# Adding three weight sums by transfers, scaling a token tile by itself, and reordering work at the output projection

## What is computed

```
h    = rms_norm(x, g_pre)                        # 512 x 2048
proj = h @ w_in                                  # 512 x 7174
out_a = moba_attention(qa, ka, va, rel_bias)     # 6 heads of 128, causal, relative bias
out_b = forgetting_attention(qb, kb, vb, log_f)  # 6 heads, bias from cumulated log forget gates
km, vm = split(rms_norm(mem, g_mem) @ w_mem_kv)  # 256 memory tokens
out_m = memory_attention(qm, km, vm)             # 4 heads
y = concat(out_a * silu(ga), out_b * silu(gb), out_m * silu(gm))
o = y @ w_out                                    # 512 x 2048 times 2048 x 2048
return x + rms_norm(o, g_post)
```

## Time and profile before

| | |
|---|---|
| median of three runs | 887.97 us |
| profiled execution | 889.66 us |
| its span on the core | 887.9 us |
| PE busy | 865.6 us, 97% |
| DVE busy | 727.2 us, 82% |
| ACT busy | 536.8 us, 60% |
| POOL busy | 75.9 us, 9% |
| mean granted clock of PE | 0.994 |

### The profile page before, as it was taken

One profiled execution on the slowest core, in us unless ns is written; L12 is line 12 of the kernel. 1 busy time (PEld: TensorE's weight loads), 2 busy tenths in 40 slices (PEclk: granted clock), 3 DMA queues, 4 the chain that ended last, 5 costly groups with the idle time before them and its releaser, 6 DMA issues.

```text
span 887.9 us, 13757 instructions
## 1 busy us (share of the span) xinstructions
PE 865.6 (97%) x5181; PEld 766.0 (86%) x5181; DVE 727.2 (82%) x1025; ACT 536.8 (60%) x918; POOL 75.9 (9%) x84
## 2 busy tenths in 40 slices
PE   9998999999999999999999999999999989999995
PEld 6997999988888888888888888888888878778884
DVE  5799789988888888888888888888888886975558
ACT  6795556565656565656565656565656575654452
POOL 0000310000000000000030303030301000000000
PEclk9999999999999999999999999999999999999999
DMA  9980586567668577657677768577644597466845
GB/s 289 303 200 23 165 181 165 148 172 159 160 171 196 137 178 176 161 163 177 153 183 170 165 171 185 144 185 170 161 121 107 172 366 259 146 214 208 289 190 189
DMA packets 179143, 161.37 MB, mean 182 GB/s; under 512 B 7353, under 2 KB 144217, under 8 KB 177670
## 3 DMA queue, kind: packets, MB, share of 16 engines
q1 hardware_dynamic: 170166, 142.66, 52.6%
q0 software_dynamic: 8704, 16.78, 13.7%
q10 hardware_dynamic: 208, 1.07, 0.4%
HBM read 152.33 MB, written 43.28 MB: 220 GB/s over the span
## 4 chain that ended last, share of the span: by engine, by line
PE 78%; DVE 12%; ACT 6%; issue 4%; DVEq 0%; POOL 0%; ACTq 0%; POOLq 0%
PE d_ps L709 19%; PE d_ps L714 10%; PE e_ps L709 10%; PE e_ps L714 5%; PE c_ps L709 5%; PE pt_ps L819 3%; DVE ring L1482 3%; PE d_ps L658 3%; PE c_ps L714 2%; PE d_ps L659 2%; PE d_ps L660 2%; ACT ring L1032 2%; PE score_ps L659 2%; PE score_ps L658 2%; PE score_ps L660 2%
## 5 line engine op out<-in xcount | busy, mean ns | idle before, releaser
L1482 DVE TENSOR_TENSOR ring<-raw,ring 128x1024 fp32r<-128x1024 f32 x134 | 164.5, 1230 | 48.6 <-ACT ring L1032 48.5
L1482 DVE TENSOR_TENSOR ring<-sums,ring 128x1024 fp32r<-128x1024 f32 x112 | 137.5, 1227 | 51.2 <-ACT ring L1032 51.1
L1032 ACT ACTIVATE ring<-raw 128x1024 fp32r<-128x1024 f32 x134 | 140.7, 1055 | 41.5 <-PE d_ps L660 15.4
L709 PE MATMUL d_ps<-late,ring 128*128 128x512 f32 x576 | 145.1, 394 | 0.0
L1032 ACT ACTIVATE ring<-sums 128x1024 fp32r<-128x1024 f32 x112 | 118.1, 1054 | 16.3 <-DVE sums L1509 13.1
L709 PEld LDWEIGHTS d_ps<-late,ring 128*128 128x128 f32 x576 | 103.4, 189 | 18.5
L714 PEld LDWEIGHTS d_ps<-late,ring 128*128 128x128 f32 x576 | 78.6, 190 | 5.7
L714 PE MATMUL d_ps<-late,ring 128*128 128x256 f32 x576 | 80.2, 282 | 0.0
L1509 DVE TENSOR_TENSOR sums<-raw 128x1024 f32<-128x1024 f32 x56 | 68.7, 1227 | 0.1
L1509 DVE TENSOR_TENSOR sums<-sums,raw 128x1024 f32<-128x1024 f32 x56 | 68.5, 1223 | 0.0
L2057 POOL DMA_DIRECT2D sum_dram<-in_w_out_dram x32 | 28.8, 900 | 421.0 <-DMA sum_dram<-in_w_out_dram 275.2
(11 more groups left out here) (387 smaller groups left out, 1915.4 us busy)
## 6 DMA issues: line engine op xcount, KB each, us to landing
raw<-in_w_in_dram SPq DMA_DIRECT2D x112, 512.0 KB, 5.7
sum_dram<-in_w_out_dram POOLq DMA_DIRECT2D x32, 512.0 KB, 7.4
raw<-sum_dram SPq DMA_DIRECT2D x32, 512.0 KB, 3.9
raw<-in_w_out_dram SPq DMA_DIRECT2D x24, 512.0 KB, 7.3
raw<-in_w_mem_kv_dram SPq DMA_DIRECT2D x16, 512.0 KB, 7.9
sum_dram<-in_w_out_dram SPq DMA_DIRECT2D x16, 512.0 KB, 6.4
sum_dram<-sum_dram SPq DMA_DIRECT2D x16, 512.0 KB, 6.1
stage<-in_x_dram SPq DMA_DIRECT2D x4, 1024.0 KB, 10.8
```

The lines of the kernel that those rows point to most:

```text
L709: pe.matmul(bank[:], w[:, 0, k], both[:, k], start=i in (TOK_A, TOK_B) and k == 0, stop=False, skip_group_check=True)
L1032: act.activation(dst, src, ACTF.Copy).then_inc(hi_done, 1)
L1482: return dve.tensor_tensor(dst, a_, hi_.bitcast(F32), ALU.subtract)
```

## The change

Three parts. **Token tiles:** the third token tile gets its root from ACT right behind its squares and is scaled by itself, earlier in DVE's queue; ACT copies the bias table out one weight operand earlier. **Sums:** the sums for B, C and E of pair 0 are no longer made by DVE. SP copies the first term of each from `raw` to `sums` inside SBUF when all tiles are turned, and POOL adds the second term (for C the third, too) by adding transfers. Two loads of pair 1 wait for the low half of E of pair 0, where they waited for the third sum. **Output projection:** the last pair's second gate half is taken ahead of a weight, the last head's probabilities are split ahead of the weights of their step, one weight is split a step later, some of the work on the gated output moves by one to three steps, and one gain and one finish at the end move by one step.

```
-ROOTS = 4
+ROOTS = 5
+FIRST_TERM = [R21, R21, R11]
-FINISH_DURING = {LAST_STEPS - SUBS + 1: (0, 2), LAST_STEPS - SUBS + 2: (1, 3)}
+GAINS_DURING = {n + (1 if n == LAST_STEPS - SUBS - 1 else 2): STEPS[n][:2] for n in range(LAST_STEPS - SUBS)
+                if n % SUBS == SUBS - 1 and STEPS[n][1] in (TOK_D, TOK_E, TOK_F, TOK_G)}
+FINISH_DURING = {LAST_STEPS - SUBS: (0, 2), LAST_STEPS - SUBS + 2: (1, 3)}
...
-    return [s for s in {0: [4], 1: [5, 6]}.get(n, [n + OUT_RING]) if s < len(STEPS)]
+    return [s for s in {0: [4], 1: [5], 2: [6, 7]}.get(n, [n + OUT_RING]) if s < len(STEPS)]
...
# SP, load(m, src): what lay in the buffer
+                    elif j == R12:
+                        sp.wait_ge(sum_done, sum_count(p, 3))
+                    elif p > 0:
+                        sp.wait_ge(sum_done, sum_count(p, 2))
                     else:
-                        sp.wait_ge(sum_done, 4 * p + (4 if j == R12 else 3))
+                        sp.wait_ge(lo_done, operand(p, TOK_E) + 1)
...
# SP, behind the four loads of pair 0
+                if p == 0:
+                    sp.wait_ge(bank_turned, 4 * TILES)
+                    for s, j in enumerate(FIRST_TERM):
+                        piece_landed(sp, 0, j)
+                        sp.dma_start(sum_tile(0, s), raw_tile(piece(0, j))).then_inc(first_loaded[s], 16)
...
# ACT
+                    if p == 0 and SUM_OF[i] < SUMS:
+                        act.wait_ge(first_sum[SUM_OF[i]], 32 if i == TOK_C else 16)
+                    else:
+                        act.wait_ge(sum_done, sum_count(p, SUM_OF[i]))
...
             squares(4)
+            root(4, 4)
...
-            root(5, 4, 2)
+            root(5, 5)
...
             hi_mem(12)
-            hi_mem(13)
             for i, (bank, lo_, hi_) in enumerate(table_banks):
...
+            hi_mem(13)
...
# ACT, output projection
-                if n in (1, 2):
-                    hi_pt(last_head, n)
...
-                if n == 17:
+                if n == 20:
                     hi_y(TOK_F)
...
+                if n in (1, 2):
+                    hi_pt(last_head, n)
                 for ahead in steps_ahead(n):
                     hi_out(STEPS[ahead])
...
# DVE
             take_keys(3)
+            scale_tile(4)
             lo_mem(10)
...
-            scale_tiles(4, 4, 2)
+            scale_tile(5)
...
             lo_operand(0, 0)
-            add_weights(0, 1)
             lo_v_mem(2)
...
             lo_v_mem(3)
-            add_weights(0, 2)
...
                     merge(p, i)
+                if (p, i) == (last_pair, TOK_G):
+                    second_strip(p, i)
...
# DVE, output projection
+                if n in (1, 2):
+                    lo_pt(last_head, n)
                 for ahead in steps_ahead(n):
                     lo_out(STEPS[ahead])
...
-                if n == 8:          # wait for y_landed[F], then the combination for C
+                if n == 7:
...
-                if n == 9:
+                if n == 8:
                     dve.wait_ge(y_sum, 2)
                     lo_y(TOK_B, 5).then_inc(y_ready, 1)
...
-                if n == 19:
+                if n == 21:
                     lo_y(TOK_F, 9).then_inc(y_ready, 1)
...
# POOL
+            def add_first(s, j):
+                piece_landed(pool, 0, j)
+                pool.dma_start(sum_tile(0, s), raw_tile(piece(0, j)), accum_op=ALU.add).then_inc(first_sum[s], 16)
+
+            pool.wait_ge(first_loaded[0], 16)
+            add_first(0, R22)
+            pool.wait_ge(first_loaded[1], 16)
+            add_first(1, R22)
+            pool.wait_ge(first_loaded[2], 16)
+            add_first(2, R21)
+            pool.wait_ge(first_sum[1], 16)
+            add_first(1, R11)
```

More of the change, by code:

```diff
@@ L344, in build @@
         sum_done = sem("sum_done")
+        first_loaded = [sem(f"first_loaded{s}") for s in range(SUMS)]
+        first_sum = [sem(f"first_sum{s}") for s in range(SUMS)]
         used = sem("used")
@@ L440, in raw_tile, with sum_count, piece_landed @@
             return raw[:, m % RAW]
+        def sum_count(p, s):
+            return 4 * p + s + 1 - SUMS
+        def piece_landed(engine, p, j):
+            m = piece(p, j)
+            engine.wait_ge(raw_landed[m % RAW], 16 * (m // RAW + 1))
         def sum_tile(p, s):
@@ L1042, in hi_operand @@
                 if i in SUM_OF:
-                    act.wait_ge(sum_done, 4 * p + SUM_OF[i] + 1)
+                    if p == 0 and SUM_OF[i] < SUMS:
+                        act.wait_ge(first_sum[SUM_OF[i]], 32 if i == TOK_C else 16)
+                    else:
+                        act.wait_ge(sum_done, sum_count(p, SUM_OF[i]))
                     src = sum_tile(p, SUM_OF[i])
@@ L1492, in add_weights @@
                 s = SUM_OF[i]
+                if p == 0 and s < SUMS:
+                    return
                 for j in {0: (R21, R22), 1: (R11,), 2: (R11, R21), 3: (R12,)}[s]:
@@ L1499, in add_weights @@
                 if s == 1:
-                    dve.wait_ge(sum_done, 4 * p + 1)
+                    dve.wait_ge(sum_done, sum_count(p, 0))
+                elif s == 3 and p == 0:
+                    dve.wait_ge(first_sum[1], 32)
                 elif s == 3:
-                    dve.wait_ge(sum_done, 4 * p + 2)
-                elif s == 0 and p > 0:
-                    dve.wait_ge(sum_done, 4 * p)
+                    dve.wait_ge(sum_done, sum_count(p, 1))
+                elif s == 0:
+                    dve.wait_ge(sum_done, sum_count(p - 1, 3))
                 one, two = {0: (raw_tile(piece(p, R21)), raw_tile(piece(p, R22))),
@@ L1536, in rstd, with scale_tile @@
                 chain(dve.tensor_tensor(stat[:, 4, c], stat[:, 2, c], stat[:, 3, c], ALU.mult))
[L1538 to L1544, removed]
+            def scale_tile(t):
+                dve.wait_ge(squares_done, t)
+                rstd(t, t)
+                one = stage[:, t % 4]
+                dve.tensor_scalar(one, one, stat[:, 4, t:t + 1], None, ALU.mult).then_inc(tile_scaled, 1)
             def lo_memory(b0, b1):
@@ L1742, in _ @@
             lo_mem(6)
-            scale_tiles(2, 2)
+            scale_tile(2)
             lo_mem(7)
-            scale_tiles(3, 3)
+            scale_tile(3)
             lo_keys(0)
@@ L1834, in after_operand @@
                     first_strip(p, i)
-                if p >= NM and i in (TOK_E, TOK_G):
+                if p >= NM and i in (TOK_E, TOK_G) and (p, i) != (last_pair, TOK_G):
                     second_strip(p, i)
@@ L1917, in y_work @@
                     lo_y(TOK_D, 3, LAST_TILE + 1, KH).then_inc(y_ready, 1)
-                if n in (1, 2):
-                    lo_pt(last_head, n)
                 if n == 4:
@@ L2008, in _ @@
                 y_work(n)
-                if n % SUBS == 1 and n > 1 and STEPS[n - 2][1] in (TOK_D, TOK_E, TOK_F, TOK_G):
-                    gain(*STEPS[n - 2][:2], 0)
-                    gain(*STEPS[n - 2][:2], 1)
+                if n in GAINS_DURING:
+                    gain(*GAINS_DURING[n], 0)
+                    gain(*GAINS_DURING[n], 1)
                 if n in FINISH_DURING:
```

## The result

| | before | after |
|---|---|---|
| median of four runs each | 888.06 us (887.89 to 889.35) | 883.27 us (882.70 to 884.55) |
| profiled execution, its span | 889.66, 887.9 us | 884.55, 882.8 us |
| mean granted clock | 0.994 | 0.993 |

The ratio is 0.9945, with an interval of 0.9930 to 0.9961: faster by 4.8 us, where 7.7 were forecast.

The account below looks back on a forecast made before the run. PE, busy 865.6 of 887.9 us, was taken as the bound, so gains lie in its few waits, half clock and tail. Front -2.3, output projection -4.3, tail -1.1 gave -7.7; with 1.69 off the profiled 889.66, 880.3 us, range 877.2 to 885.2.

Parts of the forecast that it names:

- rival 2: Pair 0: C's sum lands at 81 to 84 us, PE restarts at 85.6 to 88.6; 881.9 to 884.9; chance 0.26.
- I take 79 us for the sum of C: Pair 0's adding transfers: C's sum lands at 79 us, between 73.5 and about 83, just in time, cost nothing.
- the slow end: Pair 0's sums: four adds at 139 GB/s, 3.8 us each, end at 81.9 and land at about 83.
- The deadline: Pair 0: C's sum needed by 79.4 us, for ACT's copy before DVE reaches C's low half at 80.5.
- the -2.3 us of DVE's queue: Pair 0, ahead of product C: two removed adds of 1.14 us let PE restart at 84.0 instead of 86.28.
- The clock: After PE's wait ahead of product C, pair 0: half clock costs 2.75 us, left unchanged by the forecast.
- Rival 1: After PE's wait in pair 0: it idles only 2.3 us, the clock holds, 2.75 us saved; 877.5; chance 0.16.
- a wait of 2.3 us lies at the edge: PE's wait ahead of product C, pair 0: borderline for a clock fall, which before came 2.3 us after PE stopped.
- Output projection: -5.0 for -4.3: Output projection: four PE waits removed, forecast -1.2 (gate), -0.8 (probabilities), -1.3 (B's low half), -1.0 (F's high half), sum -4.3.
- rival 3: Output projection: moved instructions wait behind others, likely F's low half; half of 4.3 given back; 882.4; chance 0.10.
- Tail: After PE's last matmul: one finish a step earlier lets the last reduction start sooner, -1.1 us.
- rival 4: Pair 0's adding transfers run in series, landing at 94.7 us; front part costs +13.0; 895.6; chance 0.08.

Follow-up runs that it names:

- experiment 3: Changed kernel with the two loads of pair 1 held back until C's sum has landed: 880.15 us, ratio 0.9899 to the kernel before.
- experiment 6: Changed kernel with 24 unneeded matmuls filling PE's wait ahead of product C of pair 0: 881.41 us, ratio 0.9914 to the kernel before.
- experiment 7: Changed kernel with pair 1's two loads held back until C's sum landed and 8 unneeded matmuls ahead of product C: 878.27 us, ratio 0.9881.
- experiment 1: Changed kernel with the sums of pair 0 made by DVE again: 882.12 us, ratio 0.9930 to the kernel before.
- experiment 9: Changed kernel with the last head's probabilities split behind the weights again: projection stretch 157.23 us, +2.25 against 154.98.
- experiment 12: Changed kernel with the first finish at its old step: last reduction 3.31 us behind PE's last matmul against 2.19.

## Why the prediction came out as it did

The time lay in the range and the sign was right, but not by the forecast's case: what happened is rival 2, sums that come late (81 to 84 us, restart 85.6 to 88.6), which had 0.26 against 0.35. That rival named the size as well, 883.4 us in the middle.

- **The step that failed: "I take 79 us for the sum of C."** It landed at 82.90, near the slow end of 83, but not for the slow end's reason. That end counted all four adds at 139 GB/s, where 195 are reached inside SBUF, and left the loads of pair 1 out. At the right rate the four adds alone end near 77, as the prediction says itself, and without the loads the sum does land at 78.2 (experiment 3). What was missing is the loads: the forecast says that they "compete with the adds" and gives that no price, rival 2 gives it one us, and they cost 3.8 to 5.7. The copies were issued at 60.24, not at 61.2, because the last tiles were turned 1 us earlier, which makes the miss larger. The 79 was picked between two ends and not worked out, so that experiment 3 comes near it is partly luck. The Trainium skill (Collectives: The Full Stack, section on the bandwidth ceiling) states the half rate for the reduce step of a collective, whose add reads two sources where a copy reads one. The adds inside SBUF show the same here, 195 GB/s, against 397 for the plain transfers of the changed kernel from 62.5 to 65 us:
```profile
DMA packets 270, 0.99 MB, mean 397 GB/s; under 512 B 31, under 2 KB 31, under 8 KB 269
```
  For the engine time of an add inside SBUF the half of a copy's rate (2.6 us) was right and the row between DRAM tensors (3.8 us) was not; the mistake was to count that time as if nothing else were in the engines.
- **The deadline and the -2.3 us of DVE's queue were right**: in experiment 3 DVE reached C's low half at 80.54, where 80.5 was said, and PE restarted at 84.07 for 84.0. In the changed kernel the front gave +1.07 up to the anchor, 3.4 us away from the forecast.
- **The clock was left as it was, and so it was.** Its price of 2.75 us is a little high: experiment 6 gives 1.9 to 2.8, and the stretch from restart to anchor 2.4 to 2.5. Behind the wait of 2.38 us that the forecast was about, the price was 1.6 (experiment 7). Rival 1, a clock that holds at a wait of 2.3 us, probably came true in one execution of four of experiment 3 (878.13 us), so its place beside the forecast was fair. That "a wait of 2.3 us lies at the edge" was too firm: at 3.58 us it fell in the kernel before and didn't in the profile of experiment 1. What decides it is open.
- **Output projection: -5.0 for -4.3.** All four waits went and no next one came (rival 3 is out: F's halves were in time). The term is too small because it counts idle time alone. PE's idle time in the stretch fell by 4.2 us, which is the sum of the four waits; the other 0.8 are busy time, 155.76 us before and 154.91 after, as matmuls that follow each other overlap (they start every 0.23 us and are shown as 0.39 long), and a wait breaks that up. Across the gate's wait of 1.20 us the kernel before took 1.44 us longer, from one matmul's start to the next, than the changed kernel at the same place. That one wait hid a part of the next changes what each edit is worth by itself (experiment 9), not the sum of all.
- **Tail: -1.1** as forecast, and by the edit named (experiment 12).
- **Adds one after the other (rival 4) is out:** C's first add and E's were issued at 66.79 and 68.01, and C's landed at 76.69.
- **The third tile by itself** was put at nothing. Its own effect wasn't tried alone. Experiment 1 has it and restarts at 86.17 against 86.28, with DVE's sums in both, so at most 0.1 us.

## What to carry to other kernels

Work that is taken off a busy engine and given to transfers has a landing time, and that time is set by all that the transfer engines carry in those microseconds: add up the engine time of every queue in the window, the loads for later stages included, and hold back or order behind it what isn't due. Here one wait ahead of two loads, or the other order of two adds, turned a loss of 1.3 us into a gain (0.9899 and 0.9908 against 0.9930 with DVE's sums; the second by little more than the noise). When only one of several waits is removed, price the one behind it by the time at which its data is ready, not by its length in the profile; when all go, their lengths add up (here 4.2 of the 5.0 us).

## What the runs showed of the hardware

- Adding transfers inside SBUF (4 KB per partition): 192 to 200 GB/s with the 16 engines full, 2.7 us per 512 KB; between DRAM tensors it was 139 GB/s. Two and more are under way together. Two 512 KB loads beside them delayed the last of four by 3.8 to 5.7 us, and one further add ahead of it by 1.3 to 3.2.
- The landing of one and the same chain of transfers, counted from its first issue, differed by 1.9 us (21.1 to 23.0) between six executions with the loads beside it; with the loads held back it was 17.3 us both times.
- The granted clock fell behind a wait of 2.38 us in one kernel and stayed at 1.00 behind one of 3.58 us in another; where PE was kept at work it stayed at 1.00 both times. The fall cost 2.4 us (1.9 to 2.8 by the times) in the changed kernel and 1.6 us (up to 1.9 by the medians) with the shorter wait.
